# Reordering the change of layer: second root and first fill piece earlier, and a fourth unit partly multiplied inside the first loop of three layers

## The chip, the cores and the metric

The kernel runs on one core of one Trainium2 chip. The metric is the device time in microseconds. Below, PE is TensorE, DVE is VectorE, ACT is ScalarE, POOL is GpSimd and SP is the queue that issues the transfers of weights.

## What is computed

The reference runs one hidden state of 256 positions and a context of 256 positions through a first block of two layers and then a second block of two hybrid layers. Only the first block is touched here. In it each layer is made of sublayers of one form:

```python
u = _modulate(_rmsnorm(h, g_pre), shift, scale)     # h * rsqrt(mean(h^2)) * g, then * (1 + scale) + shift
...                                                 # ffn: (silu(u @ Wa) * (u @ Wb)) @ w_out; attention: softmax(q k) v @ w_out
h = h + gate * _rmsnorm(y, g_post)
```

`shift`, `scale` and `gate` come from `silu(c) @ ada_w[i] + ada_b[i]`, a product with a 1024 x 9216 matrix for each layer. The order of sublayers is feed-forward (`ffn00`), differential attention (`da`), `ffn01`, `ffn10`, neighbourhood attention (`na`), `ffn11`, and then the hybrid layers `hy0` and `hy1`. The last two sublayers' outputs are needed for the second half of the 512 columns alone, so `ffn11`, and the output side of `na`, work on 256 columns.

## The kernel before

Activations stand feature-major: 8 chunks (`DC` = 8) of 128 features by 512 positions (`T`). Each product is made of three matmuls (`product_step`, L1091 to L1093): operands are split in a high part (`uR[:, 0]`, `wh`) and a low part (`uR[:, 1]`, `wl`), and high by high, high by low and low by high are summed. A *unit* is one 128-row output over all 8 chunks, so 24 matmuls. Weights come in blocks of 256 output columns (two units) into one of two slots. SP issues the transfer of a block when the block two before it has been split (semaphore `w_lo`), ACT copies the high part (`lead`, `w_hi`), DVE subtracts for the low part (`rest`, L2527, `w_lo`), and PE waits for `w_lo` in `weights`. ACT copies over a slot only when the units of the old block are complete.

Between two sublayers lies a *change of layer*. DVE runs `residual` and PE `postnorm`. PE sums columns (L1039), DVE makes the mean square, POOL takes the root (L2338), DVE splits it in two parts (`two_parts`, L2428 and L2429), and PE spreads it over the partitions (`spread`, L955). That happens twice: a first root scales y, a second root, of the new h, scales the next sublayer's input. Then DVE runs a chain over the chunks: `scale(k)` (L2646: y times the first root), `add(k)` (L2651: h + y), `norm(k)` (L2462: h times the second root), and `low(k)` (L2473: low part of u). Between `norm(k)` and `low(k)` ACT runs `shift(k)` (L1847 and L1848), which applies scale and shift and writes the high part. `low(k)` raises `u_ready`, and PE then multiplies chunk k for three units at once (`together`). The fourth unit needs the second half of the slot 1 block, which DVE splits after the last `low` (`rest_columns(b, 1, w_lo)`, L2539); the fourth unit is then one product of 8 chunks.

Beside the main work the modulation vectors are computed in pieces. A piece is 64 narrow matmuls (`ada_mul`, L883, called a *fill* when it is put in a change of layer), a copy of the rows by ACT (`ada_out`, L1817), a transposition by PE (`ada_turn`, L894) and an addition by DVE (`ada_add`, L2393). After `ffn00`, `ffn01` and `ffn10` the change of layer has two fills, after `da` and `na` one, after `ffn11` none (there PE runs `spare` matmuls, L947). Where fills are two, the first is cut: chunks 0 to 4 ahead of the second `spread`, 5 to 7 behind it.

The transposition of the last fill of a change stands, in `ffn10` and `ffn11` (`not carries`), in `gates` between the three units of `together` and the fourth unit. In DVE's program the matching `ada_add` is the first instruction of `ffn10` and of `ffn11`; behind it come the product of the two gate halves (L3163, in `ffn11` L3142), the split of the next slot 0 block (L2527, in `ffn11` in halves, L2552) and so the `w_lo` (or `w_half`) that PE's next block waits for:

```python
if st != run[0] and st not in ADA_STAGES:
    ada_add()
...
rest(s)
```

Attention (`da_heads`, `na_heads`) starts with the same `together` and then goes by steps written out by hand; the banks of PSUM of its units are planned in `da_products` and `na_products`.

## Time and profile before

| what | value |
|---|---|
| median of 3 runs | 2321.78 us (2321.51 to 2324.17) |
| the profiled execution | 2319.09 us |
| its span, first to last instruction | 2317.3 us |
| mean granted TensorE clock | 0.995 |
| PE / PEld / DVE / ACT busy | 97% / 83% / 63% / 44% |

The profile is of one execution. Times in it count from the start of the span. "Idle before" an instruction is the time its engine did nothing ahead of it, with what ended it. PE's busy share includes waiting in its pipeline, so the places where PE stands idle are read in the timeline, at each change of layer. The first matmul after a change is at 427.32 (`da`), 715.47 (`ffn01`), 1101.24 (`ffn10`), 1476.08 (`na`), 1691.10 (`ffn11`) and 1899.77 us (`hy0`).

### The profile page before, as it was taken

The numbers are of one execution on the slowest core, as the hardware profiler recorded it, in microseconds if no ns is written. First come the engines' busy times: TensorE is split into PE (matmuls) and PEld (weight loads), VectorE is DVE, ScalarE is ACT, GpSimd is POOL, SyncE is SP. The second block draws the span as 40 slices with busy tenths as digits, with TensorE's granted clock in tenths as the row PEclk, the third lists the DMA queues.
The fourth block names the chain that finished last, engine by engine and source line by source line (L and its number), as shares of the span: only waits on it lengthen the run. The fifth ranks groups of instructions, "written<-read, shape, count | busy, mean of one in ns | idle before, by whom it ended". The sixth has DMA issues, their size and how long they took to land.

```text
span 2317.3 us, 39481 instructions
## 1 busy us (share of the span) xinstructions
PE 2249.8 (97%) x14069; PEld 1913.2 (83%) x14069; DVE 1460.8 (63%) x2101; ACT 1016.1 (44%) x1479; POOL 33.5 (1%) x35
## 2 busy tenths in 40 slices
PE   7999999999999999999999999999899999999998
PEld 5888888787777888888788888788789989889997
DVE  4874577776767872777532234776764577857765
ACT  5322234544556332225432234644554456455554
POOL 0000000000000000000000000000000000000000
PEclk9999999999999999999999999999999999999999
DMA  9664555312133653655333425442255644215321
GB/s 338 190 189 122 159 172 173 122 61 73 38 91 109 200 176 107 185 162 150 91 86 92 113 84 153 119 117 76 84 170 166 185 138 146 86 37 165 101 74 55
DMA packets 399399, 298.66 MB, mean 129 GB/s; under 512 B 13343, under 2 KB 361253, under 8 KB 399141
## 3 DMA queue, kind: packets, MB, share of 16 engines
q1 hardware_dynamic: 365322, 231.58, 34.3%
q10 hardware_dynamic: 33946, 65.35, 8.6%
q8 instruction: 81, 1.33, 0.2%
q14 instruction: 50, 0.40, 0.1%
HBM read 295.84 MB, written 1.06 MB: 128 GB/s over the span
## 4 chain that ended last, share of the span: by engine, by line
PE 83%; DVE 9%; ACT 3%; issue 3%; DMA 1%; POOL 0%; DVEq 0%; ACTq 0%; SPq 0%; POOLq 0%
PE banks L1091 24%; PE banks L1092 23%; PE banks L1093 23%; PE banks L1357 2%; ACT wh L1856 1%; DVE wl L2527 1%; DVE uR L2473 1%; DVE yT L2646 1%; PE banks L1191 1%; DVE hT L2651 1%; PE banks L1222 1%; PE banks L1308 1%; PE banks L955 1%; PE banks L1300 1%; PE banks L1039 1%
## 5 line engine op out<-in xcount | busy, mean ns | idle before, releaser
L1091 PE MATMUL banks<-uR,wh 128*128 128x512 f32 (+1 forms) x2368 | 828.2, 350 | 20.4 <-DVE uR L2473 15.6
L1092 PE MATMUL banks<-uR,wh 128*128 128x512 f32 (+1 forms) x2368 | 811.7, 343 | 0.0
L1093 PE MATMUL banks<-uR,wl 128*128 128x512 f32 (+1 forms) x2368 | 811.2, 343 | 0.0
L2527 DVE TENSOR_TENSOR wl<-wraw,wh 128x2048 fp32r<-128x2048 f32 (+2 forms) x202 | 423.8, 2098 | 323.1 <-ACTq L1784 311.8
L1856 ACT ACTIVATE wh<-wraw 128x2048 fp32r<-128x2048 f32 (+4 forms) x208 | 367.0, 1765 | 425.4 <-PE banks L1093 369.8
L1091 PEld LDWEIGHTS banks<-uR,wh 128*128 128x128 f32 x2368 | 449.4, 190 | 95.5 <-issue 21.1
L1093 PEld LDWEIGHTS banks<-uR,wl 128*128 128x128 f32 x2368 | 449.1, 190 | 52.7
L1092 PEld LDWEIGHTS banks<-uR,wh 128*128 128x128 f32 x2368 | 449.7, 190 | 49.2 <-issue 0.5
L1091 PE MATMUL banks<-gR,wh 128*128 128x512 f32 (+1 forms) x704 | 256.8, 365 | 1.5 <-DVEq L2378 1.3
L1092 PE MATMUL banks<-gR,wh 128*128 128x512 f32 (+1 forms) x704 | 255.3, 363 | 0.0
L1093 PE MATMUL banks<-gR,wl 128*128 128x512 f32 (+1 forms) x704 | 255.2, 363 | 0.0
L2432 DVE SCALAR_TENSOR_TENSOR probn<-ada_buf,silu_c,probn 128x512 f32<-128x512 f32 x308 | 207.9, 746 | 5.3 <-DVE gR L3168 5.3
L1091 PEld LDWEIGHTS banks<-gR,wh 128*128 128x128 f32 x704 | 132.8, 189 | 24.7 <-DVEq L2378 2.0
L3163 DVE TENSOR_TENSOR half<-half,banks 128x512 f32<-128x512 f32 (+1 forms) x82 | 51.9, 633 | 158.9 <-PE banks L1093 145.5
L1093 PEld LDWEIGHTS banks<-gR,wl 128*128 128x128 f32 x704 | 132.8, 189 | 20.7
L1092 PEld LDWEIGHTS banks<-gR,wh 128*128 128x128 f32 x704 | 132.9, 189 | 20.2
L2252 ACT ACTIVATE half<-banks 128x512 f32<-128x512 f32 (+1 forms) x82 | 45.8, 558 | 111.8 <-DVEq L2378 51.5
L2270 ACT ACTIVATE yT<-banks 128x512 f32<-128x512 f32 (+1 forms) x32 | 17.4, 545 | 155.5 <-PE banks L1093 155.5
L1091 PE MATMUL banks<-wh,uR 128*128 128x256 f32 x288 | 84.0, 292 | 1.1 <-DVEq L2378 1.0
L1092 PE MATMUL banks<-wl,uR 128*128 128x256 f32 x288 | 81.4, 283 | 0.0
L1093 PE MATMUL banks<-wh,uR 128*128 128x256 f32 x288 | 81.3, 282 | 0.0
L2256 ACT ACTIVATE gR<-half 128x512 f32 (+1 forms) x82 | 48.5, 592 | 53.7 <-DVEq L2378 38.8
(345 smaller groups left out, 2390.8 us busy)
## 6 DMA issues: line engine op xcount, KB each, us to landing
wraw<-in_ffn_w_in SPq DMA_DIRECT2D x176, 512.0 KB, 5.2
ada_buf<-in_ada_w ACTq DMA_DIRECT2D x24, 1280.0 KB, 6.0
wraw<-in_w_in SPq DMA_DIRECT2D x56, 512.0 KB, 4.7
wraw<-in_ffn_w_out SPq DMA_DIRECT2D x64, 384.0 KB, 4.2
wraw<-in_ffn_w_out SPq DMA_DIRECT2D x64, 320.0 KB, 4.5
ada_buf<-in_ada_w ACTq DMA_DIRECT2D x24, 768.0 KB, 4.5
wraw<-in_da_w_in SPq DMA_DIRECT2D x24, 512.0 KB, 4.6
wraw<-in_na_w_in SPq DMA_DIRECT2D x24, 512.0 KB, 4.5
```

The costliest lines, as they stand in the source:

```text
L955: ins = mm(o[:, t * P:t * P + P], column(j, t), identR[:, :], start=(j == 0), stop=(j == 1))
L1039: ins = mm(psum[b][:, t * P:t * P + STAT_W], src[:, a:a + P], by(a // CTX), start=first and t == 0, stop=last and t == (T - c0) // P - 1)
L1091: mm(o, a[0], b[0], start=first, stop=False)
L1092: mm(o, a[0], b[1], start=False, stop=False)
L1093: return mm(o, a[1], b[0], start=False, stop=last)
L1357: ins = mm(o[:, h * P:h * P + P], a, b, start=(k == 0), stop=(k == len(parts) - 1))
L1856: do(A_(wh[:, s, 0:n], wraw[:, s, 0:n], ACT.Copy), w_hi)
L2252: do(A_(half[:, s, 0:w], o[:, 0:w], ACT.Silu), silu_ready)
L2256: do(A_(gR[:, 0, bass.ds(i * 2 + s + 2 * alone[0], 1), c0:T], half[:, s:s + 1, 0:w], ACT.Copy), gh_ready)
L2432: return V.scalar_tensor_tensor(out=out_, in0=in0, scalar=scalar, in1=in1, op0=op0, op1=op1)
L2527: do(V.tensor_tensor(wl[:, s, 0:n], wraw[:, s, 0:n], wh[:, s, 0:n].bitcast(F32), ALU.subtract), w_lo)
L3163: do(V.tensor_tensor(half[:, s, 0:w], half[:, s, 0:w], o[:, 0:w], ALU.mult), free_a, free_b, gm_ready)
```

## The change

1. In `residual`, for all six changes of layer, DVE waits for the second root and splits it (`two_parts`) ahead of `scale(0)`, and `scale(1)` moves behind `norm(0)`.
2. In `postnorm`, where there are two fills, the whole first fill (64 matmuls) stands ahead of the second `spread`.
3. `together` takes four units. In `da`, `ffn01` and `ffn10` (`JOINED`) chunks 0 and 1 of the fourth unit are multiplied behind chunks 2 and 3 of the other three, and its other six chunks after the loop. For that, DVE's `rest_columns(b, 1, w_lo)` moves into the chain, behind `low(1)`, ahead of `add(3)`. In `na` and `ffn11` the fourth unit stays whole behind the loop.
4. As the fourth unit is now inside `together`, the `ada_turn` of `ffn10` and `ffn11` comes behind it rather than ahead of it.
5. In the attention layers the fourth unit uses bank 7 rather than 5, and the first use of bank 7 for the outputs of the heads waits until that unit was read.

```diff
+        JOINS, JOINED = 2, {"da": 2, "ffn01": 2, "ffn10": 2}
...
-            for n in range(-8, -5):
-                take(("unit", n), 6 if n == -6 else n + 10)
+            for n in range(-8, -4):
+                take(("unit", n), n + 12 if n >= -6 else n + 10)
...
                 if n == 2:
-                    fill_mul(st, 0, o, range(5))
+                    fill_mul(st, 0, o)
                 else:
                     spare(psum[7], 8)
                 spread(T - c0)
                 if n == 2:
-                    fill_mul(st, 0, o, range(5, DC))
                     ada_turn(turned)
...
-            def together(os, ws, rhs, waits, rhs2=None):
+            def together(os, ws, rhs, waits, rhs2=None, joined=0):
+
+                def unit(k, j):
+                    return product_step(os[j], both(ws[j // 2], k, slice(j % 2 * P, j % 2 * P + P)),
+                                        (rhs2 if j >= 2 and rhs2 else rhs)(k), k == 0, k == DC - 1)
 
                 for k in range(DC):
                     pe.wait_ge(u_ready, waits[k])
-                    ins = [product_step(o, both(ws[j // 2], k, slice(j % 2 * P, j % 2 * P + P)), (rhs2 if j == 2 and rhs2 else rhs)(k),
-                                        k == 0, k == DC - 1) for j, o in enumerate(os)]
+                    ins = [unit(k, j) for j in range(3)]
+                    if joined and k == JOINS or not joined and k == DC - 1:
+                        pe.wait_ge(w_lo, tl["w"].up())
+                    if JOINS <= k < JOINS + joined:
+                        unit(k - JOINS, 3)
+                for e in range(joined, DC):
+                    last_ = unit(e, 3)
+                ins.append(last_)
                 return ins
...
                         if m % 4 == 0:
                             if opsum.n:
                                 pe.wait_ge(o_taken, opsum.n)
+                            else:
+                                pe.wait_ge(ga_free[7], GA["unit", -5][1] + 1)
...
-                                os = [gbank()[:, 0:T - c0] for a in range(3)]
+                                os = [gbank()[:, 0:T - c0] for a in range(3 if st == run[0] else 4)]
...
                                 for ins in made:
                                     ins.then_inc(gemm_full, 1)
+                                continue
+                            if first and st != run[0]:
                                 continue
...
-                scale(0)
                 dve.wait_ge(root_ready, tl["root"].up())
                 two_parts(old, nt)
+                scale(0)
                 add(0)
-                scale(1)
...
                     norm(to, c0, streams, k, rs)
+                    if not k:
+                        scale(1)
                     if k:
                         low(to, streams, k - 1)
+                    if k == JOINS and to in JOINED:
+                        dve.wait_ge(w_hi, tl["split"].up())
+                        rest_columns(b, 1, w_lo)
                     if k + 1 < DC:
                         add(k + 1)
...
-                dve.wait_ge(w_hi, tl["split"].up())
-                rest_columns(b, 1, w_lo)
+                if to not in JOINED:
+                    dve.wait_ge(w_hi, tl["split"].up())
+                    rest_columns(b, 1, w_lo)
```

## Rows read from the trace of the kernel before

**Rows 1.** The page's part 1: engine, busy us (share), instructions

```profile
PE 2249.8 (97%) x14069; PEld 1913.2 (83%) x14069; DVE 1460.8 (63%) x2101; ACT 1016.1 (44%) x1479; POOL 33.5 (1%) x35
```

**Rows 2.** Timeline of DVE, change ffn00 to da: start, us, operation, idle before

```profile
421.46 0.16 DVE L2428 CAST rootR<-stat 128x4 fp32r<-128x4 f32 x1
...
423.17 0.68 DVE L2462 TENSOR_TENSOR yT<-hT,banks 128x512 f32<-128x512 f32 x1
...
426.48 0.69 DVE L2473 TENSOR_TENSOR uR<-yT,uR 128x512 fp32r<-128x512 f32 x1 [0.84 <-ACT yT L1848]
...
428.89 0.68 DVE L2473 TENSOR_TENSOR uR<-yT,uR 128x512 fp32r<-128x512 f32 x1
...
439.09 0.68 DVE L2651 TENSOR_TENSOR hT<-hT,yT 128x512 f32<-128x512 f32 x1
...
439.81 0.69 DVE L2462 TENSOR_TENSOR yT<-hT,banks 128x512 f32<-128x512 f32 x1
```

**Rows 3.** Timeline of POOL, ACT and PE, the same change

```profile
419.97 1.01 POOL L2338 TENSOR_TENSOR stat<-stat,lams 128x4 f32<-128x4 f32 x1 [1.72 <-DVEq L2378]
...
423.90 0.28 ACT L1817 ACTIVATE gs<-banks 128x128 f32<-128x128 f32 x1 [4.74 <-PE banks L883]
...
424.29 0.60 ACT L1847 ACTIVATE uR<-yT,mod,coefA 128x256 fp32r<-128x256 f32 x1
...
427.32 0.47 PE L1091 MATMUL banks<-uR,wh 128*128 128x512 f32 x1 [0.84 <-DVE uR L2473]
```

**Rows 4.** Timeline of DVE, change ffn11 to hy0

```profile
1896.29 1.22 DVE L2539 TENSOR_TENSOR wl<-wraw,wh 128x1024 fp32r<-128x1024 f32 x1
...
1897.75 0.48 DVE L2432 SCALAR_TENSOR_TENSOR yT<-hT,vec,banks 128x256 f32<-128x256 f32 x1 [0.24 <-DVE wl L2539]
```

**Rows 5.** Timeline of DVE and PE, change da to ffn01

```profile
714.63 0.69 DVE L2473 TENSOR_TENSOR uR<-yT,uR 128x512 fp32r<-128x512 f32 x1 [0.42 <-ACT yT L1848]
...
720.17 0.49 PE L1091 MATMUL banks<-uR,wh 128*128 128x512 f32 x1
...
731.87 0.39 PE L1091 MATMUL banks<-uR,wh 128*128 128x512 f32 x1
...
736.99 2.29 DVE L2527 TENSOR_TENSOR wl<-wraw,wh 128x2048 fp32r<-128x2048 f32 x1 [1.49 <-ACTq L1784]
...
739.47 0.49 PE L1091 MATMUL banks<-uR,wh 128*128 128x512 f32 x1
```

**Rows 6.** Timeline of PE, first scores of da

```profile
462.03 0.70 PE L1191 MATMUL banks<-big 64*128 64x256 f32 x4 [1.62 <-DVEq L2378]
```

**Rows 7.** Timeline of PE and DVE, start of ffn10

```profile
1119.71 0.27 PE L894 MATMUL banks<-cst,gs 128*128 128x128 f32 x1
...
1120.02 0.16 DVE L2393 TENSOR_TENSOR mod<-mod,banks 128x8 f32<-128x8 f32 x1 [1.20 <-PE banks L894]
...
1120.69 0.69 DVE L3163 TENSOR_TENSOR half<-half,banks 128x512 f32<-128x512 f32 x1 [0.51 <-DVE mod L2393]
...
1121.79 2.29 DVE L2527 TENSOR_TENSOR wl<-wraw,wh 128x2048 fp32r<-128x2048 f32 x1 [0.40 <-ACTq L1784]
...
1125.30 0.39 PE L1091 MATMUL banks<-uR,wh 128*128 128x512 f32 x1
```

**Rows 8.** Timeline of PE and DVE, start of ffn11

```profile
1701.22 0.27 PE L894 MATMUL banks<-cst,gs 128*128 128x128 f32 x1
...
1702.86 2.60 DVE L2552 TENSOR_TENSOR wl<-wraw,wh 128x1024 fp32r<-128x1024 f32 x2 [0.49 <-ACTq L1784]
...
1704.21 0.37 PE L1091 MATMUL banks<-uR,wh 128*128 128x256 f32 x1
...
1711.44 0.39 PE L1091 MATMUL banks<-uR,wh 128*128 128x256 f32 x1 [1.23 <-DVEq L2378]
```

**Rows 9.** Timeline of PE, head of the kernel

```profile
32.94 0.77 PE L1091 MATMUL banks<-uR,wh 128*128 128x512 f32 x1 [4.23 <-DVE uR L2473]
```

**Rows 10.** Windows: length, busy (count) by engine, clock, DMA

```profile
33.00:37.00 4.00, 4.00 (x12) 3.14 (x12) 2.38 (x4) 4.00 (x9) 0.00 (x0) 0.63 1.04 382
```

More of the change, by code:

```diff
@@ L629, in take @@
                 uses[bank] += 1
-            for n in range(-8, -5):
-                take(("unit", n), 6 if n == -6 else n + 10)
+            for n in range(-8, -4):
+                take(("unit", n), n + 12 if n >= -6 else n + 10)
             for n in DA_STEPS:
                 g, i = da_unit(n)
-                if i is not None and n >= -5:
-                    take(("unit", n), n + 10 if n < -4 else None)
+                if i is not None and n >= -4:
+                    take(("unit", n))
                 for what, after in (("stats", 3), ("spread", 4)):
@@ L658, in na_products @@
             for m in range(-8, 24):
-                bank = 6 if m == -6 else m + 10 if m < -4 else turn % 2
+                bank = m + 10 if m < -6 else m + 12 if m < -4 else turn % 2
                 turn += m >= -4
@@ L1159, in da_heads @@
                 ws = first_weights()
-                os = [ga("unit", n) for n in range(-8, -5)]
-                for ins in together(os, ws, lambda k: both(u2, k), [u0 + 2 * (k + 1) for k in range(DC)]):
+                os = [ga("unit", n) for n in range(-8, -4)]
+                for ins in together(os, ws, lambda k: both(u2, k), [u0 + 2 * (k + 1) for k in range(DC)], joined=JOINED["da"]):
                     ins.then_inc(ga_full, 1)
-                w = weights(1, DC, 256)
                 pe.wait_ge(ada_rows, tl["ada"].n)
@@ L1169, in da_heads @@
                     if i is not None:
-                        if n >= -5 and i in (0, 2, 4):
+                        if n >= -4 and i in (0, 2, 4):
                             w = weights((3 * g + i // 2) % 2, DC, 256)
-                        if n >= -5:
+                        if n >= -4:
                             o = ga("unit", n)
@@ L1175, in da_heads @@
                             j = i % 2
-                            if n >= -5:
+                            if n >= -4:
                                 product3(o, [(both(w, k, slice(j * P, j * P + P)), both(u2, k), None)
@@ L1259, in na_heads @@
                 ws = first_weights()
-                os = [unit_bank(m) for m in (-8, -7, -6)]
-                for ins in together([*os[0:2], os[2][:, 0:SEQ]], ws, lambda k: both(u2, k),
+                os = [unit_bank(m) for m in (-8, -7, -6, -5)]
+                for ins in together([*os[0:2], os[2][:, 0:SEQ], os[3][:, 0:SEQ]], ws, lambda k: both(u2, k),
                                     [u0 + 2 * (k + 1) for k in range(DC)], lambda k: both(u2, k, slice(CTX, T))):
                     ins.then_inc(ga_full, 1)
-                w = weights(1, DC, 256)
                 pe.wait_ge(ada_rows, tl["ada"].n)
@@ L1274, in na_heads @@
                         ada_turn(psum[slot])
-                    if i is not None and m >= -5:
+                    if i is not None and m >= -4:
                         if m == -4:
@@ L1293, in na_heads @@
                             pe.wait_ge(v_ready, v0 + n - 1 + 4)
+                        if n == 1:
+                            pe.wait_ge(ga_free[7], NG["unit", -5][1] + 1)
                         if it["tile"] == 0:
@@ L1697, in gates @@
                                     made = together(os, first_weights(), lambda k: both(u2, k, slice(c0, T)),
-                                                    [u0 + len(streams) * (k + 1) for k in range(DC)])
+                                                    [u0 + len(streams) * (k + 1) for k in range(DC)],
+                                                    joined=JOINED.get(st, 0))
                                 for ins in made:
                                     ins.then_inc(gemm_full, 1)
+                                continue
+                            if first and st != run[0]:
                                 continue
```

## The prediction

> **What bounds the kernel now.** I read the page first: PE is busy 97% of the span [rows 1], so only what makes PE stand idle, or removes such idle time, moves the end. Then I read the timelines of the engines at each of the six changes of layer, since the change touches nothing else, and followed what PE waits for there. In a change PE waits for DVE. The first matmul of `da` comes 0.84 us after PE had nothing left [rows 3], released by `low(0)`, which itself waited 0.84 us for ACT's `shift(0)` [rows 2]. Then DVE sets the pace: 428.89 - 426.48 = 2.41 us for each chunk (four instructions of about 0.60 us) [rows 2], while PE needs 3 x 0.69 = 2.07 us for three units. The 0.69 us for one unit and chunk comes from `ffn01`: from the start of chunk 7 to the next block are 3 + 8 steps in 739.47 - 731.87 = 7.60 us [rows 5]. The point the reader should look at next is what follows the four units: PE's next block needs a freshly split slot 0, and that chain starts when the first two units are complete, or, in `ffn10` and `ffn11`, when DVE has done its `ada_add`.
>
> **Part 1, second root sooner, and part 2, whole first fill ahead.** In the change to `da` POOL is done at 419.97 + 1.01 = 420.98 [rows 3], and DVE splits the root at 421.46 [rows 2], so 0.4 us can be gained there. Behind it stand `scale(0)`, `add(0)` and `norm(0)`, each now needing the one before it. Such a pair takes 439.81 - 439.09 = 0.72 us from start to start in place of 0.60 [rows 2]. From 421.05: 0.50 for the split, 0.71, 0.71, so `norm(0)` at 422.97, against 423.17 [rows 2]. The second `spread` must then come behind the whole fill, 24 narrow matmuls or some 0.7 us later than it could, but it still ends ahead of 422.9 (an estimate from the split and fill above). ACT's row copy at 423.90 no longer stands ahead of `shift(0)`, which started at 424.29 [rows 3]; it moves forward into ACT's idle time of 4.74 us. ACT's four instructions for chunk 0 took 426.48 - 424.29 = 2.19 us, so they would end at 425.9. DVE gets to `low(0)` at 422.97 + 0.60 + 0.60 + 0.72 + 0.60 + 0.60 = 426.09. So `low(0)` comes 0.4 us sooner. The changes to `ffn10` and `na` have the same layout: 0.4 each. In the other three PE's first fill is not cut, and ACT is not held. To `ffn01` DVE waited only 0.42 us for ACT [rows 5]; the new pairs that depend on one another put `low(0)` 0.07 us later. To `ffn11` and `hy0` DVE's chain alone sets `low(0)`: nothing to 0.1, and 0.2 us later. Bounds for part 1 and 2 in all: -1.8 (no cost for the pairs) to +0.3 us; I take -1.0.
>
> The Trainium skill ("VectorE: DVE Perf Modes", "The DRAIN you can't avoid") says that a semaphore between two DVE instructions costs nothing extra. The pair above shows 0.12 us more. By the page the three earlier starts would be worth 0.6 each, and the sum would be about 0.8 us lower.
>
> **Part 3, the joined chunks.** The split that moves into the chain costs DVE 1.22 + 0.24 = 1.46 us until its next instruction [rows 4]. It stands ahead of `low(2)`, so chunks 2 to 7 come 1.46 us later. PE gives chunks 2 and 3 four units: from the start of chunk 2 to that of chunk 7 it needs 4 + 4 + 3 + 3 + 3 = 17 steps of 0.69 plus 0.1 to restart, 11.8 us, where it took 731.87 - 720.17 = 11.70 us with DVE's pace [rows 5]. So chunk 7 starts 1.46 + 0.1 = 1.56 us later than before (counted from the same `low(0)`), and behind it PE has 9 steps rather than 11: the four units end 1.56 - 2 x 0.69 = 0.18 us *later*. The joined chunks buy nothing, since PE's spare time in the loop is 2.41 - 2.07 = 0.34 us a chunk, and the split takes away more. What is late next are the first two units, by 1.56 us, and with them ACT's copy and DVE's split of slot 0.
>
> *`ffn01`.* The chain from chunk 7 to the split's end takes 736.99 + 2.29 - 731.87 = 7.41 us, and PE's own work 7.5: they met within 0.1 us [rows 5]. Now the chain starts 1.56 + 0.07 later and PE's own work is shorter, so PE waits: 1.63 - 0.1 = +1.5 us. Below this bound lies 0.2 (if the chain had cover I don't see).
>
> *`da`.* Slot 0 is late here too, by some 0.6 us for the unit behind the four. But PE waited 1.62 us at the first scores [rows 6], for a chain of DVE that hangs on the end of the fourth unit. That wait takes in the 0.6; the fourth unit ends 0.18 - 0.4 = -0.2 us. Without that cover it would be +0.4. I take -0.2.
>
> *`na`* has no joined chunks: -0.4 us.
>
> **Part 4, the transposition behind the fourth unit.** This is the largest term. In `ffn10` DVE stood 1.20 us in `ada_add`, waiting for PE's transposition at 1119.71; from there to the end of the slot 0 split were 1121.79 + 2.29 - 1119.71 = 4.37 us, hidden by the fourth unit, for PE's next block started at 1125.30 [rows 7]. Now the transposition comes at the end of the fourth unit, at 1125.30 - 0.4 + 0.18 = 1125.1, with nothing behind it on PE to hide the 4.37. DVE can't go round `ada_add`: behind it in its program are the gate product at 1120.69 and the split [rows 7]. PE's next block: 1125.1 + 4.37 + 0.19 (from the split's end to the matmul, 739.47 - 739.28 [rows 5]) = 1129.7, so +4.4 us; 4.0 if the 0.40 us ahead of the split was ACT's. I take 4.3.
>
> *`ffn11`.* The transposition moves from 1701.22 to the end of the fourth unit, 1704.21 [rows 8]. From there: addition, product and half a split. Before, the 2.60 us for two halves began at 1702.86, 0.49 of it after a wait for ACT that now falls away [rows 8]. So 1702.86 - 1701.22 - 0.36 + 1.30 + 0.05 = 2.65 us of PE idle. Of it up to 1.23 us may come back, because PE waited that long at 1711.44 [rows 8] for a block whose transfer doesn't move; the next slot 0 transfer does move, by the full 2.65. Bounds 1.3 and 2.65, I take 2.0.
>
> **The clock.** A stand of 4.6 us in `ffn10` is longer than any in the trace but one kind: at the head PE stood 4.23 us [rows 9], and in the 4 us behind it the granted clock was 0.63 [rows 10], the 1.2 GHz level for most of it, which costs 0.37 x 4 = 1.5 us. Stands of 0.84 and 1.62 us [rows 3, 6] changed nothing. By the nearest row I add 1.5; the other bound is 0.
>
> The Trainium skill ("TensorE: Matmul & The Clock Gate", "Why this matters for your kernels") warns against such gaps between bursts, since the array then falls back to its lower clock. The head of this trace agrees.
>
> **The sum.** `da` -0.2, `ffn01` +1.5, `ffn10` +4.3 and +1.5 for the clock, `na` -0.4, `ffn11` +2.0, `hy0` +0.2: +8.9 us. The profiled execution took 2319.09 us and would take 2328.0; the median of the runs, 2.7 us above it, 2321.78, becomes **2330.7**. The bank moves of part 5 cost nothing: bank 7 is free by then, and the wait for the fourth unit's reader lies many microseconds behind it.
>
> **Rivals.**
> - *The clock holds.* If the stand in `ffn10` doesn't lower it, 1.5 us fall away: 2329.2. For it: one row alone shows a fall, and at the head PE had done only short work before. Chance 0.30.
> - *Later slack gives back the stands.* If what follows in `ffn10` and `ffn11` waits for transfers or DVE rather than PE, the 4.3 and 2.0 shrink to about a third: 2321.8 - 0.6 + 1.5 + 2.1 + 0.2 = 2325.0. For it: the wait at 1711.44 [rows 8]. Against it: PE's 97% [rows 1], and after 1125.30 no stand of PE. Chance 0.12.
> - *Faster: DVE's new place for the split is free.* If the 1.46 us fell into time in which DVE waits for ACT (0.84 us ahead of `low(0)` [rows 2]), and the transposition were not what DVE's first gate product waits for, three layers would gain 2 x 0.69 each and three changes 0.4: 2321.8 - 4.1 - 1.2 = 2316.5. It decides if PE's next block in `ffn10` starts ahead of 1125.3. Against it: the split stands behind `low(1)`, past that wait, and the 1.20 us in [rows 7] names the transposition. Chance 0.05.
> - *Worse.* The clock falls in `ffn11` too and the wait in `da` doesn't cover slot 0: 2330.7 + 1.5 + 0.6 = 2332.8. Chance 0.08.
>
> The forecast itself has 0.45.
>
> **How the numbers follow.** The range takes in the forecast, the first and the last rival, with 0.7 us for my terms: 2326.0 to 2333.5, which holds 0.83. A change of 0.2% (4.6 us) is about what a measurement of this kernel can tell from none. Slower by more than that (above 2326.4): 0.45 + 0.30 + 0.08 = 0.83, faster 0.05, within 0.12.
>
> **What the new profile would show.** Part 1: DVE's L2428 right behind POOL's end; ACT's L1817 ahead of `norm(0)` at `da`, `ffn10` and `na`. Part 3: an L2539 of 1.22 us between the second and third `low`, and the first gate activation of `ffn01` 1.6 us later after its `low(0)`. Part 4: in `ffn10` L894 behind the fourth unit, then L2393, L3163 and L2527, and PE idle over 4 us; in `ffn11` the same with over 2 us. The prediction is wrong if PE's idle time there is under 2 us, or if it is there and the end doesn't move.

## The result, and the profile after

| what | before | changed |
|---|---|---|
| median of the runs | 2321.83 us (5 runs) | 2333.8 us (5 runs, 2333.32 to 2334.55) |
| ratio, 95% interval | | 1.0052 (1.004 to 1.0063) |
| the profiled execution | 2319.09 us | 2334.55 us |
| its span and mean granted clock | 2317.3 us, 0.995 | 2332.8 us, 0.991 |

The change makes the kernel 12.0 us slower. The forecast was 2330.7 us with a range up to 2333.5: the right sign, but 3.1 us too little, and just outside the range.

The page's part 1 of the changed kernel, to be set beside [rows 1]:

```profile
PE 2253.7 (97%) x14069; PEld 1921.1 (82%) x14069; DVE 1462.7 (63%) x2101; ACT 1016.7 (44%) x1479; POOL 33.5 (1%) x35
```

The instructions are the same in number on every engine and nearly the same in busy time. What has grown is time in which PE stands (a *stand* below), and time at a lower clock. In the changed file the lines are numbered differently: `low` is L2488, `scale` L2661, `add` L2666, `norm` L2477, the split of columns L2554, of a whole slot L2542 and in halves L2567, `two_parts` L2443 and L2444, the transposition L895, `ada_add` L2408, the gate product L3183 (L3162 in `ffn11`).

**The start of `ffn10`**, PE, timeline (start, us, operation, idle before), answering to [rows 7]. The first row is the first chunk of the layer:

```profile
1104.12 0.47 PE L1091 MATMUL banks<-uR,wh 128*128 128x512 f32 x1 [2.20 <-DVE uR L2488]
...
1128.07 0.27 PE L895 MATMUL banks<-cst,gs 128*128 128x128 f32 x1
1132.63 0.79 PE L1091 MATMUL banks<-uR,wh 128*128 128x512 f32 x1 [4.29 <-DVEq L2393]
1133.22 0.63 PE L1092 MATMUL banks<-uR,wh 128*128 128x512 f32 x1
...
1137.48 0.59 PE L1093 MATMUL banks<-uR,wl 128*128 128x512 f32 x1
1137.91 0.40 PE L1091 MATMUL banks<-uR,wh 128*128 128x512 f32 x1
```

DVE in the same stretch:

```profile
1128.38 0.16 DVE L2408 TENSOR_TENSOR mod<-mod,banks 128x8 f32<-128x8 f32 x1 [6.69 <-PE banks L895]
1129.05 0.69 DVE L3183 TENSOR_TENSOR half<-half,banks 128x512 f32<-128x512 f32 x1 [0.51 <-DVE mod L2408]
1130.15 2.29 DVE L2542 TENSOR_TENSOR wl<-wraw,wh 128x2048 fp32r<-128x2048 f32 x1 [0.40 <-DVE half L3183]
```

The transposition stands behind the fourth unit, DVE stood 6.69 us for it, and addition, gate product and split then run with nothing on PE: 4.29 us of standing. Behind it PE's matmuls take 0.63 us where they take 0.40 from 1137.91 on. The granted clock by windows (length, busy of PE, PEld, DVE, ACT and POOL, clock, share and GB/s of DMA):

```profile
1130.00:1134.00 4.00, 1.37 (x3) 1.16 (x4) 3.15 (x3) 3.14 (x3) 0.00 (x0) 0.63 0.03 8
1134.00:1138.00 4.00, 4.00 (x11) 3.06 (x10) 3.22 (x3) 0.63 (x1) 0.00 (x0) 0.51 0.92 254
1138.00:1142.00 4.00, 4.00 (x19) 3.28 (x18) 0.30 (x1) 0.60 (x1) 0.00 (x0) 1.00 0.88 245
```

0.51 is the 1.2 GHz level for all of a window. PE gets 11 matmuls done in four microseconds there, and 19 in the next four.

**The start of `ffn11`**, PE and then DVE, answering to [rows 8]:

```profile
1701.61 0.36 PE L1091 MATMUL banks<-uR,wh 128*128 128x256 f32 x1 [0.84 <-DVE uR L2488]
...
1714.73 0.27 PE L895 MATMUL banks<-cst,gs 128*128 128x128 f32 x1
1717.55 0.39 PE L1091 MATMUL banks<-uR,wh 128*128 128x256 f32 x1 [2.54 <-DVEq L2393]
...
1818.82 0.39 PE L1091 MATMUL banks<-uR,wh 128*128 128x256 f32 x1 [0.69 <-DVEq L2393]
...
1883.67 0.39 PE L1091 MATMUL banks<-gR,wh 128*128 128x256 f32 x1 [0.94 <-DVEq L2393]
```

```profile
1715.04 0.16 DVE L2408 TENSOR_TENSOR mod<-mod,banks 128x8 f32<-128x8 f32 x1 [3.40 <-PE banks L895]
...
1716.21 2.60 DVE L2567 TENSOR_TENSOR wl<-wraw,wh 128x1024 fp32r<-128x1024 f32 x2 [0.33 <-DVE half L3162]
```

The block behind the four units starts 15.94 us after the first chunk; before it was 1704.21 and 1691.10, 13.11 us [rows 8] (the first chunk's start stands in the table of the profile before). The two waits further on, of 0.69 and 0.94 us, each for a freshly split slot, had no match in the trace before.

**The change from `ffn00` to `da`**, DVE, answering to [rows 2]:

```profile
422.49 0.17 DVE L2443 CAST rootR<-stat 128x4 fp32r<-128x4 f32 x1 [0.38 <-POOL stat L2353]
422.69 0.16 DVE L2444 TENSOR_TENSOR rootR<-stat,rootR 128x4 fp32r<-128x4 f32 x1
423.00 0.69 DVE L2661 TENSOR_TENSOR yT<-yT,banks 128x512 f32<-128x512 f32 x1
423.72 0.69 DVE L2666 TENSOR_TENSOR hT<-hT,yT 128x512 f32<-128x512 f32 x1
424.52 0.69 DVE L2477 TENSOR_TENSOR yT<-hT,banks 128x512 f32<-128x512 f32 x1
...
427.65 0.69 DVE L2488 TENSOR_TENSOR uR<-yT,uR 128x512 fp32r<-128x512 f32 x1
...
430.65 1.22 DVE L2554 TENSOR_TENSOR wl<-wraw,wh 128x1024 fp32r<-128x1024 f32 x1
```

The wait of 0.84 us ahead of `low(0)` is gone, and the three first instructions stand 0.72 and 0.80 us apart where independent ones stand 0.60.

**Two yardsticks.** Executions of one kernel differ: the first chunk of `da` came at 427.32 in one profile of the kernel before and at 428.77 in another, and the stretch `na` took 1.3 us more in the second. So whole times and starts are poor measures of a microsecond. Two others repeat to 0.02 us in the two traces of the kernel before and in one of it with spare matmuls. One is the time from POOL's second root to the first chunk of the layer; before, in the change to `da`, 427.32 - 419.97 = 7.35 us [rows 3]. The other is the time from the first chunk to the block behind the four units. (Once, in the change to `ffn10` of `root_narrow`, the clock fell inside a change; that value is 8.05 and is left out.) For longer parts the length of a layer is used, from its first chunk to that of the next:

| length, us | `ffn01` | `ffn10` | `na` | `ffn11` |
|---|---|---|---|---|
| before | 385.77 | 374.84 | 215.02 | 208.67 |
| before, another execution | +0.02 | +0.01 | +1.30 | +0.12 |
| changed | +1.15 | +6.83 | +0.81 | +4.71 |

### The profile page after: what moved, and what is told of

It is laid out like the page before. It is cut to its first block, busy times and chain, and to the rows that moved or that the text cites. A ratio compares the mean times of both kernels' runs of the same rounds, so it can differ in the third digit from the quotient of the medians.

```text
span 2332.8 us, 39483 instructions
## 1 busy us (share of the span) xinstructions
PE 2253.7 (97%) x14069; PEld 1921.1 (82%) x14069; DVE 1462.7 (63%) x2101; ACT 1016.7 (44%) x1479; POOL 33.5 (1%) x35
## 4 chain that ended last, share of the span: by engine, by line
PE 82%; DVE 9%; issue 3%; ACT 3%; DMA 1%; POOL 0%; DVEq 0%; ACTq 0%; SPq 0%; POOLq 0%
PE banks L1091 24%; PE banks L1092 23%; PE banks L1093 23%; PE banks L1369 2%; DVE wl L2542 2%; ACT wh L1871 2%; PE banks L1200 1%; DVE yT L2661 1%; DVE hT L2666 1%; DVE uR L2488 1%; PE banks L1320 1%; PE banks L1233 1%; PE banks L1312 1%; PE banks L1040 1%; PE banks L904 1%
## 5 line engine op out<-in xcount | busy, mean ns | idle before, releaser
L2542 DVE TENSOR_TENSOR wl<-wraw,wh 128x2048 fp32r<-128x2048 f32 (+2 forms) x202 | 423.8, 2098 | 320.6 <-ACTq L1799 309.0
L3183 DVE TENSOR_TENSOR half<-half,banks 128x512 f32<-128x512 f32 (+1 forms) x82 | 52.0, 634 | 164.7 <-PE banks L1093 152.9
```

What stands on the lines that cost most here:

```text
L2542: do(V.tensor_tensor(wl[:, s, 0:n], wraw[:, s, 0:n], wh[:, s, 0:n].bitcast(F32), ALU.subtract), w_lo)
L3183: do(V.tensor_tensor(half[:, s, 0:w], half[:, s, 0:w], o[:, 0:w], ALU.mult), free_a, free_b, gm_ready)
```

## The experiments

Medians are compared with those of the kernel before on the same chip in the same sitting: 2322.3, 2321.8, 2321.9 and 2321.9 us in the four sittings, from 20 to 33 runs each. Intervals of a ratio reach about 0.09% (2 us) to each side with 10 or 11 runs of the kernel, and 0.14% (3 us) with 5. Each trace is of one execution, which can lie over 1 us from the median of its kernel.

### The transposition back in its place

```diff
 def together(..., joined=0, between=None):
...
+                if between:
+                    between()
                 for e in range(joined, DC):
                     last_ = unit(e, 3)
...
-                            if s and first and st != run[0] and not carries:
-                                ada_turn()
```

`ada_turn` is passed as `between`, so PE transposes between the three units and the rest of the fourth. All else is as changed.

> The changed kernel with one edit undone: in ffn10 and ffn11 the transposition of the last fill stands again between the three units and the (rest of the) fourth unit. Theory (the late transposition holds DVE, DVE holds the split of slot 0, PE stands, and the clock falls behind the stand): the stands of 4.3 us in ffn10 and 2.5 us in ffn11 go, and with them the low clock behind the first (2.6 us); what is left is about +1.5 us in ffn01, so 2324 to 2325.5 us, +2.5 against before. Rival (joining the chunks costs most, in all three layers): it stays above 2329. Rival (slack elsewhere): little comes back, above 2331.

Measured: 2325.8 us, ratio 1.0015 (1.0006 to 1.0024). By medians the late transposition costs 8.0 us of the 12.0. By length `ffn10` is 0.26 us longer than before and `ffn11` 0.95, in place of 6.83 and 4.71, which makes 10.3. The two profiled executions explain most of the difference: that of the changed kernel lies 0.75 us above its median (2334.55), that of this one 1.0 below (2324.78). DVE in `ffn10`:

```profile
1123.02 0.16 DVE L2408 TENSOR_TENSOR mod<-mod,banks 128x8 f32<-128x8 f32 x1 [2.58 <-PE banks L895]
1123.69 0.69 DVE L3183 TENSOR_TENSOR half<-half,banks 128x512 f32<-128x512 f32 x1 [0.51 <-DVE mod L2408]
1124.78 2.29 DVE L2542 TENSOR_TENSOR wl<-wraw,wh 128x2048 fp32r<-128x2048 f32 x1 [0.40 <-ACTq L1799]
```

The same chain, but it ends at 1127.07 and PE's next block starts at 1127.27: the chain is as long as the six steps of the fourth unit that now cover it.

### The joined chunks taken out

```diff
-        JOINS, JOINED = 2, {"da": 2, "ffn01": 2, "ffn10": 2}
+        JOINS, JOINED = 2, {}
```

> The changed kernel with no layer joined: the split of the second half of slot 1 goes back behind the chain in da, ffn01 and ffn10, and the fourth unit is whole; the transposition stays behind the fourth unit. Theory: only the 1.5 us of ffn01 comes back, 2331.5 to 2333 us. Rival (joining is the main cost): below 2327.

Measured: 2333.2 us, 1.0047 (1.0034 to 1.0061), 0.6 us below the changed kernel, less than the expected 1.5 but within the noise of 5 runs. The length of `ffn01` falls from +1.15 to -0.23 us: the joined chunks cost 1.4 us there. In `ffn10` the length falls by 0.75 us, but by only 0.16 between the next kernel and `turn_back`, so little is shown for it; in `da` nothing is seen.

### Both together: only the root and the fill are left

> Both edits: what is left of the change is the second root sooner and the whole first fill ahead of the second spread. Theory: 0.4 us less in each of da, ffn10 and na, about nothing in ffn01 and ffn11, 0.2 more in hy0, so 2320.5 to 2322, the same as before within what can be told. Rival (the longer stand of PE ahead of the first chunk, 2.2 us in place of 0.8, lowers the clock there and takes the gain back): 2322 to 2324, with the granted clock under 1 right behind 1101 or 1476 us.

Measured: 2324.3 us, 1.0009 (1.0000 to 1.0018). Parts 1 and 2, forecast to gain 1.0, come out 2.0 us slower, and 1.5 us below `turn_back`, which is what the joined chunks cost. The rival met the direction: the clock fell from 1105.2 us on, behind the stand ahead of `ffn10`. That the fall is the cause is tested below, and isn't borne out. This was the unexpected result, and the next runs go after it.

### The kernel before once more

> The kernel before, unchanged, for a second trace of it: which parts of the difference between the two traces at hand are between executions. All theories: 2321 to 2324 us. If the 1.4 us by which the changed kernel's trace was late ahead of the first changed instruction is chance, this trace's first matmul of da lies up to 1.5 us from 427.3; the lengths of the stages behind it agree with the first trace within 0.3 us, but for ffn11, where I expect up to 1 us.

Measured: 2322.45 us. Its trace gave the yardsticks above: `da` began 1.45 us later, as allowed for, but the layer that differed most was `na` (+1.30 us) and not `ffn11` (+0.12). The runs of the kernel before also show what most of this spread goes with: of the 33 beside the next two kernels, 10 had a mean granted clock of 0.992 and took 2322.9 us on average, 6 had 0.996 and took 2320.8.

### The fill alone, and the root alone

The first is the kernel before with part 2 of the change, the second the kernel before with part 1.

```diff
 # the fill alone
-                    fill_mul(st, 0, o, range(5))
+                    fill_mul(st, 0, o)
...
-                    fill_mul(st, 0, o, range(5, DC))
 # the root alone
-                scale(0)
                 dve.wait_ge(root_ready, tl["root"].up())
                 two_parts(old, nt)
+                scale(0)
                 add(0)
-                scale(1)
...
                     norm(to, c0, streams, k, rs)
+                    if not k:
+                        scale(1)
```

> The kernel before with part 2 alone: the whole first fill ahead of the second spread. ACT's copy of the rows no longer holds shift(0) in da, ffn10 and na. Theory: the first chunk comes 0.2 to 0.4 us sooner in these three, and PE, with all its fills done earlier, stands 1.5 to 2.2 us ahead of it in place of 0.8; where the granted clock then falls, 1 to 1.7 us are lost each time. Net against before: 0 to +2 us. Rival (forecast on record: the clock only matters behind stands over 4 us): -0.5 to -1 us, no low clock within 10 us behind 427, 1101 and 1476.

> The kernel before with part 1 alone: the second root split ahead of scale(0), scale(1) behind norm(0). Theory: the pairs that depend on one another eat the gain; low(0) comes 0 to 0.3 us later in each change, so 0 to +1 us in all. Rival (DVE is free to go on, no price for the pairs): -1 us.

Measured: the fill alone 2319.9 us, 0.9990 (0.9981 to 0.9999); the root alone 2324.2 us, 1.0008 (0.9999 to 1.0017). The fill is the good part, the root the bad one. The fill gained more than its theory and its rival had it (-1.9 us, against 0 to +2 and -0.5 to -1), and the root lost more (+2.4 us, where 0 to +1 was expected). A different mean clock isn't the root's reason: at the same one the kernel with the root is the slower one too, with 2324.2 against 2322.9 us at 0.992 (4 and 10 executions) and 2323.3 against 2320.8 at 0.996 (3 and 6). From POOL's second root to the first chunk of each layer, in us:

| | `da` | `ffn01` | `ffn10` | `na` | `ffn11` | `hy0` |
|---|---|---|---|---|---|---|
| before | 7.35 | 6.95 | 7.35 | 7.35 | 4.54 | 6.42 |
| fill alone | 6.95 | 6.95 | 6.95 | 6.94 | 4.55 | 6.42 |
| root alone | 7.11 | 7.15 | 7.11 | 7.11 | 4.82 | 6.76 |
| changed | 7.11 | 7.15 | 7.12 | 7.11 | 4.82 | 6.76 |

The fill alone takes 0.40 us out of each of three changes. Its ACT in the change to `da`:

```profile
422.04 0.28 ACT L1816 ACTIVATE gs<-banks 128x128 f32<-128x128 f32 x1 [2.75 <-PE banks L883]
424.02 0.60 ACT L1846 ACTIVATE uR<-yT,mod,coefA 128x256 fp32r<-128x256 f32 x1 [1.71 <-DVE yT L2461]
```

The row copy has moved into idle time of ACT, so `shift(0)` starts with `norm(0)` and no longer behind the copy. With the root moved as well, `norm(0)` ends earlier, but `low(0)` stands behind a longer row of DVE instructions, and 0.16 us of the 0.40 are lost; in the three changes in which nothing was to be gained, 0.20, 0.28 and 0.34 us are simply added.

The traces show two further places that this table leaves out. In `ffn10`, with the early root, the block behind the four units comes 24.4 us after the first chunk (24.41 in `root_only`, 1126.98 - 1102.57; 24.40, 24.39 and 24.38 in three more kernels with nothing joined and the transposition in its place), where it is 24.05 before and 24.04 with the fill alone. So in `ffn10` 0.36 us are lost behind the first chunk, more than the 0.24 won ahead of it; `ffn01` has 24.0 either way. And `ffn11` is longer: 209.3 to 211.8 us, median 210.1, in the six traces with the root early there and the transposition in its place, against 208.7 to 209.6, median 208.9, in the seven without it. The later change to `hy0` makes 0.34 of these 1.2 us.

A fall of the clock behind these stands does not show in the lengths: with the fill alone it fell behind the stand ahead of `ffn10` in one trace and not in the other (`fill_again`, below), and the layer took 374.42 and 374.41 us.

### The clock held through the changes of layer

PE stands 2.2 us ahead of the first chunk in the changed kernel where it stood 0.84 us before, and the clock fell behind some of these stands. In both kernels here spare matmuls (128x512, 0.23 us each) stand behind the last fill; the first has parts 1 and 2 alone, the second is the kernel before.

```diff
                 if n:
                     fill_mul(st, n - 1, o)
+                    spare(psum[...], MORE[to])   # 4 to 7 of them with parts 1 and 2, 2 to 6 in the kernel before
```

> The kernel with parts 1 and 2 only (transposition in its old place, nothing joined), and spare matmuls on PE behind the last fill: 7 at da, ffn10 and na, 6 at ffn01, 4 more at hy0, each 0.23 us, into the time in which PE stood. Theory: PE's clock no longer falls behind the changes of layer, and the 0.4 us per change show: 1 to 2 us under before, 2320 to 2321.5, with clock 1.00 from 1101 to 1120 and 1476 to 1496. Rival (the gain of 0.4 us isn't there): as before or slower, 2322 to 2325.

> The kernel before with spare matmuls in the same place, as many as fit its shorter stands: 2 at da, ffn10 and na, 6 at ffn01, 3 more at hy0. It tells what keeping the clock is worth by itself. Theory: the fall behind 715 us, seen in most traces but the first, goes: 0.5 to 1.5 us under before. Rival (falls are ruled by something else): same as before.

Measured: 2324.7 us, 1.0012 (1.0003 to 1.0021), and 2321.95 us, 0.9997 (0.9988 to 1.0006). In the profiled execution the falls behind the changes of layer are gone and the mean clock is 0.997, but over all runs it rose only from 0.992 to 0.994 with parts 1 and 2, since the clock also falls elsewhere. The medians did not gain: the kernel with parts 1 and 2 is 2.95 us above the kernel before with the spares, and was 2.0 above it without them. The low clock behind those stands is not what parts 1 and 2 cost. For `before_held` the rival holds as well. The trace of `before_again` agrees: the clock fell behind the stand ahead of `ffn01`, as it did not in the first trace, and the layer took 385.79 us against 385.77. In these first microseconds DVE sets the pace, and PE has time to spare.

### The root in narrow or in wide changes alone

The order of part 1 is chosen by `c0`: in the first kernel it is new for the changes to `ffn11` and `hy0` alone (256 columns), in the second for the other four, together with the fill.

> Kernel before with the earlier second root in the changes to ffn11 and hy0 alone (256 columns). Part 1 everywhere cost +2.4 us. Theory A (its cost sits in the narrow changes, where the dependent pairs of DVE take longer and DVE alone sets the first chunk, and the later start makes later transfers of weights late): +1.8 us, 2323.6, with the first chunk of ffn11 0.4 to 0.5 us later and further 1 us in the waits for transfers in ffn11. Theory B (its cost sits in the wide changes, where the second root's early split moves the head of the chain): within 0.3 us of before.

> Kernel before with the whole first fill ahead of the second spread, and the earlier second root only in the changes to da, ffn01, ffn10 and na (512 columns). Theory A (the two parts together free 0.4 us each in da, ffn10 and na, as forecast, and the narrow changes were what cost): 2319.3, about 0.5 us below the kernel with the fill alone (2319.9). Theory B (the wide changes lose by the root too): above 2320.5.

Measured: 2323.6 us, 1.0009 (1.0000 to 1.0018), and 2322.9 us, 1.0006 (0.9997 to 1.0015). The narrow changes cost: 4.81 and 6.75 us by the yardstick, +0.27 and +0.33. But the second kernel is 3 us above the fill alone where its four changes show 3 x 0.16 + 0.21 = 0.7, so for the second kernel theory B holds: the wide changes lose by the root too. For the first kernel the median meets theory A's number, but by another way: its first chunk of `ffn11` is 0.27 us late and not 0.4 to 0.5. The further waits in `ffn11` that A spoke of were absent in the narrow kernel's trace and one, of 0.88 us, was there in the wide one's, whose `ffn11` starts as before:

```profile
1693.43 0.36 PE L1090 MATMUL banks<-uR,wh 128*128 128x256 f32 x1 [0.31 <-DVE uR L2472]
...
1872.33 0.38 PE L1090 MATMUL banks<-gR,wh 128*128 128x256 f32 x1 [0.88 <-DVEq L2377]
```

These waits come and go from trace to trace (one of 0.68 us stands in the kernel before with its clock held as well), so no single one can be put down to part 1. They are more frequent with it, though: waits of 0.7 to 2 us in the second half of `ffn11` stand in five of the six traces with the early root there, and in two of the seven without it. Why is not shown.

### The fill with the joined chunks, without the root

> Changed kernel without the earlier root and with the transposition back between the three units and the fourth: the whole first fill ahead, and the joined chunks with the split in the chain. Theory A (parts add up: fill -1.9, joined chunks +1.5 from ffn01): 2321.4 beside 2321.8 of before. Theory B (joined chunks cost nothing or gain once the root is left out): 2320 or less.

Measured: 2321.6 us, 0.9999 (0.9990 to 1.0008). Theory A: what the fill gains, the joined chunks give back; `ffn01` is +0.99 us, where it is -0.38 with the fill alone. Its 0.3 us under the kernel before are within the noise.

### The clock held behind the late transposition

```diff
                             if s and first and st != run[0] and not carries:
                                 ada_turn()
+                                spare(psum[4], 9 if c0 else 17)
```

> Changed kernel with narrow spare matmuls on PE behind the transposition, 17 in ffn10 and 9 in ffn11, into a bank that no unit uses then, so that PE does not stand while DVE adds, multiplies the gates and splits. Theory A (2.6 us of ffn10's 6.6 and about 1 us of ffn11's are the clock that fell behind the stand): first block behind the four units comes as late as in the changed kernel, granted clock 1.00 behind it in both layers, 2330.5. Theory B (the lag comes from elsewhere, the low clock only goes along): 2333.8 as the changed kernel.

Measured: 2332.5 us, 1.0042 (1.0028 to 1.0056), 1.3 us below the changed kernel, between the theories, a difference that 5 runs each don't tell from none; what the clock costs is read from the traces. PE in `ffn10`:

```profile
1103.32 0.47 PE L1091 MATMUL banks<-uR,wh 128*128 128x512 f32 x1 [2.19 <-DVE uR L2489]
...
1127.20 0.27 PE L895 MATMUL banks<-cst,gs 128*128 128x128 f32 x1
1127.22 4.15 PE L948 MATMUL banks<-identR 128*128 128x512 f32 x17
1131.75 0.49 PE L1091 MATMUL banks<-uR,wh 128*128 128x512 f32 x1 [0.38 <-DVEq L2394]
...
1134.60 0.39 PE L1091 MATMUL banks<-uR,wh 128*128 128x512 f32 x1
```

The block comes 1131.75 - 1127.20 = 4.55 us behind the transposition, as in the changed kernel (1132.63 - 1128.07 = 4.56), so the spares delay nothing. The spares here are 17 of 128x512, not narrow as the text put on record calls them. The next 12 matmuls take 2.85 us, against 1137.91 - 1132.63 = 5.28 in the changed kernel: the low clock costs 2.4 us in `ffn10`. In `ffn11`, held at full clock too, nothing came back by the end of the layer. It took 214.07 us (1913.28 - 1699.21), +5.4, against +4.7 in the changed kernel. PE was faster there at first. The block behind the one just shown (it waited 1.23 us and started at 1711.44 before [rows 8]) starts 21.79 us after the first chunk, against 23.27 in the changed kernel and 20.34 before; the first row below is of this kernel, the second of the changed one:

```profile
1721.00 0.28 PE L1091 MATMUL banks<-uR,wh 128*128 128x256 f32 x1
1724.88 0.28 PE L1091 MATMUL banks<-uR,wh 128*128 128x256 f32 x1
```

Then it waited longer for its slots:

```profile
1699.21 0.35 PE L1091 MATMUL banks<-uR,wh 128*128 128x256 f32 x1 [0.83 <-DVE uR L2489]
...
1727.27 0.38 PE L1091 MATMUL banks<-uR,wh 128*128 128x256 f32 x1 [0.35 <-DVEq L2394]
...
1815.83 0.38 PE L1091 MATMUL banks<-uR,wh 128*128 128x256 f32 x1 [0.97 <-DVEq L2394]
...
1889.85 0.38 PE L1091 MATMUL banks<-gR,wh 128*128 128x256 f32 x1 [1.48 <-DVEq L2394]
...
1913.28 0.36 PE L1091 MATMUL banks<-uR,wh 128*128 128x256 f32 x1 [1.77 <-DVE uR L2489]
```

Two more traces say the same of `ffn11`: the clock fell behind its stand in `late_ffn11` (next section) and not in `unjoined`, and the layer took 212.33 and 212.37 us.

### The transposition late in one layer alone

The changed kernel with `between=ada_turn` in `ffn11` alone (late in `ffn10`), and in `ffn10` alone (late in `ffn11`).

> Changed kernel with the transposition late in ffn10 alone; in ffn11 it is back between the three units and the fourth. Theory A (each layer pays for itself: 6.6 us in ffn10, of it 4.0 stand and 2.6 low clock): 4 us below the changed kernel, 2330.0, and ffn11 as long as in turn_back. Theory B (all of it is ffn10's and later slack in ffn11 hides its own): 2333 or more.

> Changed kernel with the transposition late in ffn11 alone. Theory A (each layer pays for itself; in ffn11 the stand of 2.5 us, and waits for weights that its late split makes later): 3.8 us above turn_back, 2329.6. Theory B (only what the forecast took, 2.0 us, the rest of ffn11's lag follows from ffn10): 2327.8.

Measured: 2330.2 us, 1.0037 (1.0023 to 1.0051), and 2327.7 us, 1.0024 (1.0015 to 1.0034). (The changed kernel and `turn_back` are from other sittings, which adds up to 0.5 us of doubt to the differences.) Late in `ffn10` adds 4.4 us to the kernel with the transposition in its place and, seen from the other side, taking it away in `ffn10` saves 6.1; the trace says 6.3 (`ffn10` +6.55, less 0.26). Late in `ffn11` adds 1.9 from the one side and 3.6 from the other; the trace says 2.7 (+3.66, less 0.95). Each layer pays for itself, with the larger part in `ffn10`; theory B of `late_ffn10` (2333 or more) is out. For `ffn11` the median meets theory B's number and the trace lies between A and B.

### The fill alone once more

> Kernel before with the whole first fill ahead of the second spread, once more, beside the runs above. Theory A (0.40 us in each of three changes of layer, as the traces show from the second root to the first chunk): 1.2 us below before, 2320.6. Theory B (also later waits fall away, as the first 1.9 us would have it): 2319.9 or less. Rival: no difference, the first result was chance.

Measured: 2320.0 us, 0.9994 (0.9985 to 1.0003), again 1.9 us below before, with the same 6.94 and 6.95 us by the yardstick. That is near theory B; the yardstick gives 1.2 us, and where the other 0.7 would come from isn't shown. Of the kernels run this is the fastest; by each interval alone its gain is at the edge of what can be measured.

## Why the prediction was off

The mechanism of the largest term was right. The steps that failed are terms of the sum: parts 1 and 2 (-1.0 forecast, +2.0 by medians), the clock in `ffn10` (1.5 against 2.4) and `ffn11` (2.0 against 2.7 to 3.8 in the traces).

- **The late transposition, mechanism and place: right.** DVE's `ada_add` waits for it, and product and split are uncovered. In `ffn10` the block behind the four units came 28.51 us after the first chunk (1132.63 - 1104.12), against 24.06 [rows 7], +4.45 us, or +4.2 with the 0.24 that the change of layer gained. The forecast had +4.3. `turn_back` shows it as a cause.
- **The clock, a term mis-sized: 1.5 forecast, 2.4 measured** (`after_held`). The row taken as the nearest, the head of the kernel, had a window of 0.63 [rows 10]; here one of 0.51 followed behind one of 0.63, so the low stretch was about twice as long. The head had been read nearly in full: the windows on both sides of [rows 10] have 0.94 and 1.00. But it was read in one execution, and the length differs between executions at the same place. In the changed kernel's own head, which no edit touches:

```profile
32.00:36.00 4.00, 2.74 (x7) 2.19 (x8) 3.46 (x6) 4.00 (x9) 0.00 (x0) 0.50 1.05 386
36.00:40.00 4.00, 4.00 (x55) 2.96 (x57) 1.67 (x3) 2.95 (x4) 0.00 (x0) 0.65 1.04 387
```

That the head is the one row with a fall was a misreading as well. In the same trace of the kernel before the clock falls in `da`, where PE, between short products, stands no longer than 1.04 us at a time:

```profile
633.00:637.00 4.00, 2.96 (x13) 2.18 (x12) 3.31 (x9) 2.84 (x8) 1.01 (x1) 0.54 0.00 0
637.00:641.00 4.00, 3.08 (x16) 2.94 (x15) 3.31 (x9) 0.70 (x4) 0.00 (x0) 0.50 0.00 0
```

- **`ffn11`, a term mis-sized: 2.0 forecast, 2.7 to 3.8 in the traces and 1.9 to 3.6 by medians.** The lateness of the block is 15.94 - 13.11 = 2.83 us, near the 2.65 worked out. That the wait of 1.23 us [rows 8] would give part of it back was right only with the clock held: the block that had this wait is 1.45 us late in `after_held` and 2.93 in the changed kernel, where the clock fell here too, from about 1718 on, behind a stand of only 2.54 us. The forecast had no clock term for `ffn11`, and it took no later wait into account: slots are waited for again at 1818.82 and 1883.67 (ahead of the first, ACT's copy waited 1.65 us, until 1814.42, for the transfer). `after_held` shows that the two stand in for each other: with the clock up, PE waits for slots instead, and the layer ends no sooner. The fall in `ffn11` was in the rival "Worse".
- **Parts 1 and 2, the step that failed by sign.** Forecast -1.0 us. By the yardstick the six changes give 3 x (-0.24) + 0.20 + 0.28 + 0.34 = +0.1, and the medians +2.0. The 0.4 us in three changes were forecast for both parts together, which gave 0.24; that the fill alone gives 0.40 is luck, since it was never worked out alone. The error is in the root: the pairs that depend on one another take up to 0.80 us, not 0.72, the split of the root starts 0.11 us behind POOL rather than 0.07, and in the changes without anything to gain the cost is 0.20 and 0.28 where 0.07 and nothing to 0.1 were taken. The Trainium skill ("VectorE: DVE Perf Modes", "The DRAIN you can't avoid") has a semaphore between two DVE instructions cost nothing extra; the rows of `da` above differ from it by 0.12 to 0.20 us, and the measurement decides. Of the 1.9 us between +0.1 and +2.0, the traces place 0.36 in `ffn10`, behind the first chunk, and about 0.9 in `ffn11` (1.2 less the 0.34 of the change to `hy0`); the forecast had nothing in either place. The rest is no wider than the interval of the median. Why the two layers get longer stays open; a different mean clock is not the reason.
- **The joined chunks in `ffn01`: right.** The chain over the chunks is 734.00 - 716.36 = 17.64 us long, where it was 16.27, 1.37 more (1.46 forecast), and the block behind the four units comes 742.57 - 717.19 = 25.38 us after the first chunk, where it was 739.47 - 715.47 = 24.00 [rows 5]: +1.4, with +1.5 forecast. "The joined chunks buy nothing" holds.
- **`da`, `na` and the banks: right in size.** In `da` the first scores come 34.72 us after the first chunk, as before within 0.01 (462.03 - 427.32 [rows 3, 6]), so that only the 0.24 us of the change of layer are gained. The cover was as forecast: PE's wait there shrank from 1.62 to 0.97 us. In `na` 0.24 us were gained, where 0.4 was forecast. The moved banks have no run of their own; `da` takes 288.7 us in the changed kernel and with the fill alone, where they are not moved.
- **The range.** Its upper end, 2333.5, follows from the rivals (2332.8 + 0.7). Its lower end does not: 2329.2 - 0.7 is 2328.5 and not 2326.0. The terms for `ffn11` add up to 2.63 rather than 2.65. Neither moves the forecast.

Set right, the sum is -0.2 (`da`), +1.6 (`ffn01`), +4.2 and +2.4 (`ffn10`), -0.2 (`na`), +2.7 to +3.8 and 0.3 (`ffn11`), +0.3 (`hy0`): 11.1 to 12.2 us, against 12.0 measured. This is put together from single profiles. The medians share the same 12.0 out differently: 8.0 for the late transposition, 1.5 for the joined chunks, 2.0 for parts 1 and 2. That the first sum meets the 12.0 does not settle the open part.

## What to carry to other kernels

An instruction of one engine that a second engine waits for can be the first link of a chain three engines long: before moving it behind other work, add up everything that is queued behind the waiting instruction, and ask what still covers it. If a stand is long enough to lower the clock, look for every low stretch in the trace and in a second execution, since one example gives neither the shortest stand nor the length of the stretch; and ask whether PE sets the pace behind it, since otherwise the fall costs nothing. Taking a wait away by a new order pays only where that wait ended last: the fill took away such a wait, while the root's earlier split mostly made three independent instructions depend on one another.

## What the runs showed of the hardware that was not expected

- The granted clock fell to the 1.2 GHz level behind stands of PE as short as 2.54 us (`ffn11`), 2.19 us (`na`) and 2.11 us, in the change to `ffn01` of the changed kernel:

```profile
717.19 0.47 PE L1091 MATMUL banks<-uR,wh 128*128 128x512 f32 x1 [2.11 <-DVE uR L2488]
...
717.97 0.54 PE L1091 MATMUL banks<-uR,wh 128*128 128x512 f32 x1
718.30 0.63 PE L1092 MATMUL banks<-uR,wh 128*128 128x512 f32 x1
```

It did not fall behind the 2.20 us ahead of `ffn10` in that trace (it did behind 2.18 us there in `unjoined`). In another execution of the kernel before it fell behind the 1.90 us ahead of `ffn01`, and in the first one it did not. Ahead of the stands at `na` and `ffn01` PE had done the narrow matmuls of the fills, ahead of the one in `ffn11` full products. The Trainium skill ("TensorE: Matmul & The Clock Gate", "Why this matters for your kernels") advises against idle gaps between bursts of matmuls only from a length that none of these reaches; here shorter ones were enough, and the measurement decides.
- 128x512 DVE instructions that depend on the one before start 0.72 or 0.80 us after it, independent ones 0.60 (the rows of `da` above).
- Holding the clock up bought 2.4 us, by the traces, where PE was the bound (`ffn10`), and nothing where the split of late weights was (`ffn11`, 214.07 us held and 213.38 not).
- A fall of the clock where DVE sets the pace cost nothing: `ffn01` took 385.77 us without and 385.79 with one, `ffn10` 374.41 and 374.42.
